# One small constant tile cut from 16 columns to 1, in a two-layer hybrid decoder trunk

## The chip, the cores and the metric

The kernel runs on one core of one Trainium2 chip. The metric is the device time of one execution, in microseconds (us), lower is better; the times shown are medians over several executions.

## The reference, cut to what matters

Two layers. Layer 0 mixes tokens with a chunked state-space scan, layer 1 with causal pooling windows. Each layer is followed by a gated feed-forward block with a causal depthwise convolution. Every sub-layer stands between two RMS normalisations. All is float32, 512 tokens of 1024 features.

```python
def rms_norm(x, w):
    xf = x.astype(jnp.float32)
    xf = xf * lax.rsqrt(jnp.mean(xf * xf, axis=-1, keepdims=True) + EPS)
    return (xf * w.astype(jnp.float32)).astype(x.dtype)
...
    for i in range(DEPTH):
        h = rms_norm(x, norm_mix_pre[i])
        ...
        x = x + rms_norm(mix, norm_mix_post[i])
        f = conv_ffn(rms_norm(x, norm_ffn_pre[i]), ffn_w_up[i], ffn_conv_w[i], ffn_conv_b[i],
                     ffn_w_down[i])
        x = x + rms_norm(f, norm_ffn_post[i])
```

The group norm inside the scan mixer uses the same EPS. The constant EPS = 1e-6 is what the changed tile holds.

## The kernel before

**Work and staging.** The weights stream through in slabs of 1 MB (8 KB per partition). SyncE loads a slab into `raw`. ScalarE copies it, rounded, to `w_hi` (line 261), VectorE subtracts to get the remainder `w_lo` (line 266), and TensorE multiplies in three passes, hi by hi, hi by lo and lo by hi, to keep float32 accuracy. The input projection, the gate and the up projections are `block_product` (lines 269 to 271), with slices of the weights as the stationary operand and `h_hi`/`h_lo` moving. The output and down projections are `rows_chunk` (line 874), where the stationary operand is `y_hi`/`y_lo` or `act_hi`/`act_lo` and the weights move.

**Stages in order of time.** Start and B/C projection (0 to 95 us of the profile), the scan over 16 head pairs (95 to 310), output projection (310 to 390), normalisations (390 to 435), up projection of layer 0 (435 to 666), down (666 to 764), normalisations and pooling mixer (764 to 843), up of layer 1 (843 to 1074), down (1074 to 1194), last normalisation and store. Every engine has a program written out by hand, in a fixed order, tied to the others by semaphores.

**The steps of the scan that the text names.** For each head pair: transposes of `xbc` (line 600), twelve products of `xde` and `cb_off` (line 646), sixteen of `xdt` and `decay` (line 655). `decay` is loaded by a DMA (line 547), then changed in place by VectorE (line 779), ScalarE (lines 694 and 699) and VectorE (`mask_dve`, line 786), which the products of line 655 wait for. Once for each group of four pairs there are the products of line 573. The normalisations transpose `stage` on TensorE (line 333). The causal taps of the convolutions are line 380: each reads a bank of PSUM and adds into `tmp[:, slot, back:]` with `back` 1, 2 or 3, so that the operand in SBUF begins 4, 8 or 12 bytes behind the start of its slot; the three forms are told apart by their lengths, 511, 510 and 509.

**The tile `eps`.** It is allocated as `[P, 16]`, filled once by GpSimd (line 1152), and read as `eps[:, 0:1]`, the bias of the square roots of lines 291, 314 and 730. Columns 1 to 15 are read by nothing. TensorE and ScalarE wait at the start for the four constants, of which it is one.

**Where tiles lie.** Tiles are placed in the order in which they are declared, one behind the other, and the start of each is rounded up to a multiple of 32 bytes per partition. In the compiled kernel before, `eps` lies at byte 118,400 of each partition and takes 64 bytes. All the tiles of the kernel, before and behind it, have sizes that are multiples of 64 bytes, and all begin at multiples of 64. Ahead of it lie `xres`, `h_hi`, `h_lo`, `raw`, `w_hi`, `w_lo`, `par`, `ident`, `upper` and `ones`. Behind it lie `tmp`, `pre_b`, `post_b`, the small tiles of the norms, the pooling windows, `xbc` and everything that shares memory with it in turn: `cb_diag`, `cb_off`, `xdt`, `xde`, `decay`, `from_start`, `gate`, `y_hi`/`y_lo`, `act_hi`/`act_lo`, `wf_hi`/`wf_lo`, `stage`, `wdt_*`. The sharing is by stacked scopes and by filler tiles of fixed size, all behind `eps`.

Of the kernel before, what the change touches and what calls it, by code (L numbers as in the profile page):

```python
# [10 lines left out]
P = 128  # L11
# [5 lines left out]
def hybrid_trunk(nc, x, ssd_w_in, ssd_conv_w, ssd_conv_b, ssd_dt_bias, ssd_a_log, ssd_d, ssd_norm_w,  # L17
# [75 lines left out]
    with ExitStack() as ctx:  # L93
        def sb(name, shape, dt=F32, scope=ctx):
            return scope.enter_context(nc.sbuf_tensor(name, shape, dt))
# [15 lines left out]
        ident = sb("ident", [P, P])  # L111
        upper = sb("upper", [P, P])
        ones = sb("ones", [P, P])
        eps = sb("eps", [P, 16])
        tmp = sb("tmp", [P, 4, T])
        pre_b = sb("pre_b", [P, D])
        post_b = sb("post_b", [P, D])
# [1353 lines left out]
```

## Time and profile before

| | |
|---|---|
| median of 3 runs | 1201.6 us (1200.21 to 1202.83) |
| the profiled execution's own time | 1202.83 us |
| its span, first to last instruction | 1201.1 us |
| PE / PEld / DVE / ACT / POOL busy | 96% / 81% / 56% / 44% / 3% |
| granted TensorE clock, mean | 0.987 of full |

The profiled execution is the slowest of the three runs, and its span is 1.7 us shorter than its time. PE is TensorE's matmuls, PEld its weight loads (they overlap the matmuls), DVE VectorE, ACT ScalarE, POOL GpSimd, and SPq the queue of SyncE, which issues the loads. In an engine's column "busy" counts instructions at work; a wait is told by the instruction that came late.

### The profile page before, as it was taken

To read this page: it belongs to the slowest core of one execution; us is meant where nothing else is said; L and a number is where in the kernel's file an instruction comes from. 1 tells how busy PE (TensorE), PEld (TensorE's weight loads), DVE (VectorE), ACT (ScalarE), POOL (GpSimd) and SP (SyncE) were. 2 spreads that over 40 slices of the span, in tenths; PEclk is the share of its full clock that TensorE was granted. 3 is DMA by queue.
4 is the path that set the end of the run, shared out by engine and by line. 5 is a ranking of instruction groups with operands and counts; after the bars stand their busy time and mean duration, and the time that the engine had idled before them with its cause. 6 is when DMAs were issued, how large, how long until landed. Compare 5 with 4: busy or idle time off the path is not lost.

```text
span 1201.1 us, 14740 instructions
## 1 busy us (share of the span) xinstructions
PE 1155.5 (96%) x5780; PEld 972.4 (81%) x5780; DVE 671.8 (56%) x766; ACT 523.0 (44%) x613; POOL 32.6 (3%) x87
## 2 busy tenths in 40 slices
PE   5999999999999899999999999998999999999997
PEld 5877888888788688888888888898888888888886
DVE  4567777878732746556565422466556566652124
ACT  4467666667532544434444211354434434441112
POOL 5000000000100000000000000000000000000000
PEclk9999999999999899999999999988999999999999
DMA  8142343433222303333222322402232332223211
GB/s 277 57 139 79 123 132 117 130 116 133 102 70 105 106 10 134 103 105 102 88 89 105 105 105 99 164 1 70 87 102 75 105 105 90 88 102 105 105 70 70
DMA packets 85227, 122.26 MB, mean 102 GB/s; under 512 B 4150, under 2 KB 71198, under 8 KB 85182
## 3 DMA queue, kind: packets, MB, share of 16 engines
q1 hardware_dynamic: 84592, 121.37, 30.1%
q8 instruction: 33, 0.54, 0.2%
q10 hardware_dynamic: 590, 0.25, 0.1%
q14 instruction: 12, 0.10, 0.0%
HBM read 119.44 MB, written 2.16 MB: 101 GB/s over the span
## 4 chain that ended last, share of the span: by engine, by line
PE 89%; DVE 5%; ACT 3%; DMA 1%; issue 1%; SPq 0%; DVEq 0%; ACTq 0%
PE bank L874 25%; PE bank L269 19%; PE bank L271 19%; PE bank L270 19%; PE bank L646 2%; DVE w_lo L266 2%; PE bank L655 1%; ACT w_hi L261 1%; DMA raw<-in_ssd_w_in 1%; DVE stage L301 1%; DVE xres L304 1%; PE bank L1035 1%; PE bank L600 1%; PE bank L333 1%; PE bank L573 1%
## 5 line engine op out<-in xcount | busy, mean ns | idle before, releaser
L269 PE MATMUL bank<-h_hi,w_hi 128*128 128x512 f32 (+1 forms) x1056 | 404.4, 383 | 11.1 <-DVE h_lo L345 7.7
L271 PE MATMUL bank<-h_hi,w_lo 128*128 128x512 f32 (+1 forms) x1056 | 400.2, 379 | 0.0
L270 PE MATMUL bank<-h_lo,w_hi 128*128 128x512 f32 (+1 forms) x1056 | 400.0, 379 | 0.0
L266 DVE TENSOR_TENSOR w_lo<-raw,w_hi 128x2048 fp32r<-128x2048 f32 x92 | 210.8, 2292 | 238.5 <-ACT w_hi L261 238.2
L380 DVE SCALAR_TENSOR_TENSOR tmp<-bank,par,tmp 128x511 f32<-128x511 f32 (+2 forms) x248 | 185.2, 748 | 129.4 <-ACT tmp L371 116.6
L261 ACT ACTIVATE w_hi<-raw 128x2048 fp32r<-128x2048 f32 x92 | 175.4, 1906 | 169.5 <-PE bank L874 152.3
L269 PEld LDWEIGHTS bank<-h_hi,w_hi 128*128 128x128 f32 x1056 | 201.5, 191 | 49.6 <-DVE w_lo L266 7.3
L271 PEld LDWEIGHTS bank<-h_hi,w_lo 128*128 128x128 f32 x1056 | 201.2, 191 | 36.8
L270 PEld LDWEIGHTS bank<-h_lo,w_hi 128*128 128x128 f32 x1056 | 201.6, 191 | 35.4
L371 ACT ACTIVATE tmp<-bank,par 128x512 f32<-128x512 f32 x112 | 86.8, 775 | 259.5 <-PE bank L271 259.3
L874 PE MATMUL bank<-w_hi,act_hi 128*128 128x512 f32 x352 | 109.1, 391 | 0.0
L874 PE MATMUL bank<-w_hi,act_lo 128*128 128x512 f32 x352 | 108.8, 390 | 0.0
L874 PE MATMUL bank<-w_lo,act_hi 128*128 128x512 f32 x352 | 108.8, 390 | 0.0
L874 PEld LDWEIGHTS bank<-w_hi,act_hi 128*128 128x128 f32 x352 | 66.5, 189 | 13.8
L874 PEld LDWEIGHTS bank<-w_hi,act_lo 128*128 128x128 f32 x352 | 66.4, 189 | 13.8
L874 PEld LDWEIGHTS bank<-w_lo,act_hi 128*128 128x128 f32 x352 | 66.4, 189 | 13.8
L993 ACT ACTIVATE act_hi<-tmp 128x512 f32 (+1 forms) x44 | 27.3, 634 | 58.6 <-DVE tmp L1008 58.6
L874 PE MATMUL bank<-w_hi,y_hi 128*128 128x512 f32 x128 | 40.8, 400 | 2.0 <-DVE w_lo L266 2.0
L874 PE MATMUL bank<-w_lo,y_hi 128*128 128x512 f32 x128 | 39.9, 394 | 0.0
L874 PE MATMUL bank<-w_hi,y_lo 128*128 128x512 f32 x128 | 39.8, 392 | 0.0
L990 ACT ACTIVATE tmp<-tmp 128x512 f32<-128x512 f32 x44 | 27.4, 627 | 25.6 <-DVE tmp L380 25.6
L345 DVE TENSOR_TENSOR h_lo<-bank,h_hi 128x512 fp32r<-128x512 f32 x32 | 20.7, 684 | 27.3 <-ACT h_hi L339 27.3
(161 smaller groups left out, 973.9 us busy)
## 6 DMA issues: line engine op xcount, KB each, us to landing
raw<-in_ffn_w_up SPq DMA_DIRECT2D x44, 1024.0 KB, 5.0
raw<-in_ffn_w_down SPq DMA_DIRECT2D x22, 1024.0 KB, 4.8
raw<-in_ssd_w_in SPq DMA_DIRECT2D x20, 1024.0 KB, 5.7
decay<-ac_dram SPq DMA_DIRECT2D x16, 512.0 KB, 3.8
raw<-in_ssd_w_out SPq DMA_DIRECT2D x8, 1024.0 KB, 4.9
from_start<-ac_dram SPq DMA_DIRECT2D x32, 128.0 KB, 3.7
xres<-in_x SPq DMA_DIRECT2D x4, 512.0 KB, 7.9
result<-xres SPq DMA_DIRECT2D x4, 512.0 KB, 2.6
```

The lines of the kernel that those rows point to most:

```text
L261: act.activation(w_parts(n, i)[0][:], raw[n % 2][:], ACT.Copy).then_inc(hi_ready, 1)
L266: dve.tensor_tensor(lo[:], raw[n % 2][:], hi[:].bitcast(F32), ALU.subtract).then_inc(lo_ready, 1)
L269: pe.matmul(dst, wh, xh, start=first, stop=False, **kw)
L270: pe.matmul(dst, wh, xl, start=False, stop=False, **kw)
L271: return pe.matmul(dst, wl, xh, start=False, stop=last, **kw)
L345: dve.tensor_tensor(h_lo[:, 4 * j:4 * j + 4, cs(c)], chunked(bank[:, 2 * c + j, :]), h_hi[:, 4 * j:4 * j + 4, cs(c)].bitcast(F32), ALU.sub ...
L371: act.activation(tmp[:, slot, :], bank[:, source, :], ACT.Identity, bias=b, scale=w).then_inc(conv_tap, 1)
L380: dve.scalar_tensor_tensor(tmp[:, slot, back:], bank[:, source, 0:T - back], w, tmp[:, slot, back:], ALU.mult, ALU.add).then_inc(conv_part ...
L646: mm = pe.matmul(bank[:, YO_BANK, cs(c)], xde[:, i, :], cb_off[p // QPG % 2][:, i, :], start=i == froms[0], stop=i == froms[-1])
L874: mm = pe.matmul(bank[:, 2 * c + j, :], x[:, cs(c)], w[:, k, j * T:(j + 1) * T], start=start, stop=stop)
L990: act.activation(tmp[:, j, :], tmp[:, j, :], ACT.Silu).then_inc(gate_silu, 1)
L993: act.activation(act_hi[:, bass.ds(2 * i + j, 1), :].rearrange("p a l -> p (a l)"), tmp[:, 2 + j, :], ACT.Copy).then_inc(act_hi_ready, 1)
```

## The change

`eps` becomes one column wide. The memset of line 1152 then writes one column. Nothing else in the source changes: not an instruction, a semaphore, a loop or a transfer. As the starts are rounded up to 32 bytes, `eps` takes 32 bytes in place of 64, and every tile behind it begins 32 bytes earlier: at 32 past a multiple of 64 instead of on one. All of them move by the same amount, so which tiles share memory stays as it was, and the ten named tiles ahead of `eps` don't move.

```diff
@@ -111,7 +111,7 @@
         ident = sb("ident", [P, P])
         upper = sb("upper", [P, P])
         ones = sb("ones", [P, P])
-        eps = sb("eps", [P, 16])
+        eps = sb("eps", [P, 1])
         tmp = sb("tmp", [P, 4, T])
         pre_b = sb("pre_b", [P, D])
         post_b = sb("post_b", [P, D])
```

## Rows read from the trace of the kernel before

**Rows 1.** The page: busy time of each engine, and the chain that ended last.

```profile
PE 1155.5 (96%) x5780; PEld 972.4 (81%) x5780; DVE 671.8 (56%) x766; ACT 523.0 (44%) x613; POOL 32.6 (3%) x87
...
PE 89%; DVE 5%; ACT 3%; DMA 1%; issue 1%; SPq 0%; DVEq 0%; ACTq 0%
PE bank L874 25%; PE bank L269 19%; PE bank L271 19%; PE bank L270 19%; PE bank L646 2%; DVE w_lo L266 2%; PE bank L655 1%; ACT w_hi L261 1%; DMA raw<-in_ssd_w_in 1%; DVE stage L301 1%; DVE xres L304 1%; PE bank L1035 1%; PE bank L600 1%; PE bank L333 1%; PE bank L573 1%
```

**Rows 2.** Windows, scan and last down projection: PE, PEld, DVE, ACT, POOL, clock, DMA.

```profile
95.00:310.00 215.00, 215.00 (x1244) 179.75 (x1246) 168.77 (x228) 146.10 (x166) 12.96 (x10) 1.00 0.37 121
...
1074.00:1194.00 120.00, 119.80 (x529) 98.90 (x527) 34.88 (x25) 26.77 (x24) 0.00 (x0) 1.00 0.23 85
```

**Rows 3.** Timeline of the first microseconds: start, duration, engine, line.

```profile
0.95 0.11 POOL L1152 MEMSET eps<- 128x16 f32 x1
...
2.90 0.10 POOL L1165 MEMSET win_first<- 128x1 f32 x1
...
4.79 1.28 ACT L312 ACT_TABLE_LOAD   x1 [4.79 <-DMA xres<-in_x]
```

**Rows 4.** Groups by line and form on VectorE: busy us, mean ns, idle before.

```profile
L380 DVE SCALAR_TENSOR_TENSOR tmp<-bank,par,tmp 128x510 f32<-128x510 f32 x112 | 83.9, 749 | 12.0 <-DVE tmp L380 2.7
L380 DVE SCALAR_TENSOR_TENSOR tmp<-bank,par,tmp 128x511 f32<-128x511 f32 x112 | 83.6, 746 | 116.6 <-ACT tmp L371 116.6
...
L1008 DVE TENSOR_TENSOR tmp<-tmp 128x512 f32<-128x512 f32 x44 | 28.3, 684 | 0.0
...
L304 DVE TENSOR_TENSOR xres<-xres,stage 128x1024 f32<-128x1024 f32 x16 | 19.6, 1225 | 0.6
L779 DVE TENSOR_TENSOR decay<-a_cum,decay 128x1024 f32<-128x1024 f32 x16 | 19.6, 1223 | 6.1 <-DMA decay<-ac_dram 6.1
L786 DVE TENSOR_TENSOR decay<-decay,cb_diag 128x1024 f32<-128x1024 f32 x16 | 19.5, 1219 | 0.9 <-ACT decay L699 0.9
...
L380 DVE SCALAR_TENSOR_TENSOR tmp<-bank,par,tmp 128x509 f32<-128x509 f32 x24 | 17.9, 748 | 0.8
...
L816 DVE SCALAR_TENSOR_TENSOR tmp<-xbc,d_pair,bank 128x512 f32<-128x512 f32 x16 | 11.9, 743 | 0.0
...
L819 DVE TENSOR_TENSOR tmp<-tmp 128x384 f32<-128x384 f32 x16 | 8.9, 558 | 0.5
```

**Rows 5.** One line on ScalarE: duration ns min/median/max, first and last start, form.

```profile
L314 ACT ACTIVATE rms_x<-ss_x,eps x16: 294/296/298, 8.6 to 829.9; 128x1 f32<-128x1 f32 x16
```

**Rows 6.** Weight load and matmul of line 874: duration ns min/median/max.

```profile
L874 PEld LDWEIGHTS bank<-w_hi,act_hi x352: 187/188/333, 665.9 to 1192.3; 128*128 128x128 f32 x176
L874 PE MATMUL bank<-w_hi,act_hi x352: 387/389/774, 666.1 to 1192.5; 128*128 128x512 f32 x176
```

**Rows 7.** The chain near the end: start us, us, what.

```profile
1149.83 43.99 PE bank L874 x194
```

**Rows 8.** The chain in the scan and at a transpose: start us, us, what.

```profile
101.01 1.34 PE bank L646 x12
102.34 1.02 PE bank L655 x16
...
109.05 0.44 PE bank L600 x4
...
136.95 2.16 PE bank L573 x8
...
426.39 0.87 PE bank L333 x8
```

**Rows 9.** DMA issues: KB each, median us from issue to landing.

```profile
decay<-ac_dram SPq DMA_DIRECT2D x16, 512.0 KB, 3.8
```

**Rows 10.** Timeline of one step of the scan: DVE, and PE's start on decay.

```profile
108.51 1.23 DVE L779 TENSOR_TENSOR decay<-a_cum,decay 128x1024 f32<-128x1024 f32 x1 [2.48 <-DMA decay<-ac_dram]
...
113.74 1.23 DVE L786 TENSOR_TENSOR decay<-decay,cb_diag 128x1024 f32<-128x1024 f32 x1 [0.19 <-ACT decay L699]
...
116.23 1.09 PE L655 MATMUL bank<-decay,xdt 128*64 128x128 f32 x16
```

## The prediction, made before the changed kernel ran

> **What bounds the kernel now.** I read the page first: TensorE's matmuls are busy for 96% of the span, and the chain that ended last lies on TensorE for 89% of it, on VectorE for 5% and on ScalarE for 3% [rows 1]. So a change of the time has to come through TensorE's own instructions, or through the 8% in which TensorE is waiting for a chain of VectorE and ScalarE work (the start, the normalisations between the stages, the tail). Then I read the windows by stage. In the scan TensorE is busy for all of its 215.00 us, VectorE for 168.77 and ScalarE for 146.10; in the last down projection TensorE is busy for 119.80 of 120.00 us and VectorE for 34.88 [rows 2]. VectorE and ScalarE could be slower there and nothing would show.
>
> **The change in two parts.** The source loses 15 columns that nothing reads. What can be felt is (a) a shorter memset and (b) that every tile declared behind `eps` begins 32 bytes earlier, at 32 past a multiple of 64. All instructions, their shapes, their order and their semaphores stay.
>
> (a) The memset of 16 columns takes 0.11 us, and a memset of one column 0.10 [rows 3], so 0.01 us goes. It lies at 0.95 us, while ScalarE's first work stands behind the first load of x until 4.79 us [rows 3], and TensorE's behind that. The cover is that load; if it were gone, the part would be worth 0.01 us. I take 0.
>
> (b) No row of before shows a large operand at 32 past 64. The price has to be bounded by the nearest rows, engine by engine.
>
> *VectorE.* Line 380 is the nearest, because its SBUF operand, read and written, begins 4, 8 and 12 bytes behind a multiple of 64: 746 ns for 511 elements, 749 for 510, 748 for 509. Line 816 is the same kind of instruction (one source in PSUM, one in SBUF) at a multiple of 64: 743 ns for 512 [rows 4]. An element costs (684 - 558) / 128 = 0.98 ns, from lines 1008 and 819, both in `tmp` [rows 4]. Brought to 512 elements the taps take 747, 751 and 751 ns, 4 to 8 ns over 743, at most 1.1%. Those are stranger starts than the one that comes, and the difference may be the code's own. Second, pairs of tiles: line 304 works on `xres` with `stage`, line 779 on `a_cum` with `decay`, line 786 on `decay` with `cb_diag`, and they take 1225, 1223 and 1219 ns for the same 1024 elements [rows 4]. The places of two operands against each other are worth at most 0.5%.
>
> *ScalarE.* Line 314 writes single columns of a small tile, one after another at steps of 4 bytes, and takes 294 to 298 ns in all 16 [rows 5]. That is a weak witness, since the tile is one column wide; I let VectorE's 1.1% stand as the upper end for ScalarE as well.
>
> What of it is on the path: of the chain's 8% on these two engines, 5% + 3% = about 96 us, the splits of the weights (lines 266 and 261, 2% + 1% on the page, about 36 us) work on tiles that don't move. Of the other 60 us, 1.1% is 0.7 us. The bounds are 0 and +0.7 us from the taps, and 0.5% either way, 0.3 us, from the pairs. I take 0, since a tap at 4 bytes and one at 8 differ by as much as either from an aligned one.
>
> *TensorE.* The big moving operands, `h_hi`, `h_lo`, `w_hi` and `w_lo`, lie ahead of `eps` and stay. What moves is the stationary operand of line 874 (`y_*`, `act_*`), those of a few first blocks (`wf_*`), and both operands of the short products of the scan and the transposes. For line 874 a load takes 188 ns [rows 6], and a matmul follows its predecessor every 43.99 us / 194 = 227 ns [rows 7], so a load has 39 ns, 21%, to grow in before the matmuls feel it. I know of no row with a stationary or moving operand halfway into 64 bytes. The lower bound is 0. For the upper one I suppose that TensorE reads in pieces of 64 bytes, an assumption: a row of 128 floats, 512 bytes, is 8 pieces from an aligned start and 9 from 32 bytes in, one eighth more. Line 874's load would take 212 ns and still be hidden under 227. The short products are not hidden; worked out under the rivals, they would add 8.0 us. I take 0 here too: nothing in the rows shows such a piece size, and every row in which an address phase can be seen, on the two other engines, shows at most 1.1%.
>
> *Loads into moved tiles.* `decay` lands 3.8 us after its issue [rows 9], and in one step VectorE waited 2.48 us for it; the mask of line 786 then ended at 113.74 + 1.23 = 114.97, and the products that wait for it began at 116.23 [rows 10]. So a load may land 1.26 us later, a third of its 3.8 us, before TensorE feels it. I take nothing for the loads.
>
> The Trainium skill has a rule on just this, on the page "DMA: Bandwidth & Descriptors", section "How a descriptor splits into AXI transactions": a descriptor that doesn't start at a multiple of 256 bytes pays for a whole first transaction. It tempts one to price a moved tile as dearer. But `decay` lay at 128 past a multiple of 256 before and lies at 96 past one after, so by that page its row of 4 KB goes from 132 beats to 131, which is an estimate of 1% off a transfer of 3.8 us and no loss. No row here shows a beat, and neither the sum nor a chance goes by it.
>
> **The sum.** 0.00 (memset) + 0.0 (VectorE and ScalarE) + 0.0 (TensorE) + 0.0 (loads) on the profiled execution's 1202.83 us. That one is the slowest of the three runs shown, 1.2 us over their median of 1201.6, for no reason that the change touches, so the forecast goes to the median: 1201.6 us.
>
> **The rivals.**
>
> *TensorE reads a half-shifted row slower: slower than before.* Places: each of the 16 steps of the scan has 1.34 us of line 646, 1.02 of line 655 and 0.44 of line 600 on the chain, 2.80 x 16 = 44.8 us; the four groups have 2.16 us each of line 573, 8.6 us; the three normalisations whose `stage` is transposed do so in four chunks each, 12 in all, at 0.87 us for the 8 transposes of line 333, 10.4 us [rows 8]. Together 63.8 us with nothing to hide behind, since TensorE is busy for the whole scan [rows 2]. One eighth more is 8.0 us, 1209.6 us. It decides from 2.4 / 63.8 = 3.8% more per product. For it: no row excludes it. Against it: it needs a piece size that nothing shows, and line 646 takes 1.34 us / 12 = 112 ns for 128 columns [rows 8], 0.87 ns each, where line 874 takes 227 / 512 = 0.44 ns [rows 7]: the short products get a column at half the pace at which columns are seen to come, so there is room for a longer read. In a harder form the loads of line 874 grow past 39 ns; there are 352 of them for each of the three passes of the two down projections [rows 6], 1056 in all, so that each nanosecond beyond costs 1.1 us.
>
> *A late load: slower.* If loads into tiles at 32 past 64 took half as long again, `decay` would land 1.9 us later, 0.64 us past the slack of 1.26. TensorE would stand 0.64 us in such steps; six of the sixteen loads made VectorE wait before, by 6.1 us in all [rows 4], so 3.8 us, 1205.4 us. It decides from about a third more, 1.26 us plus 0.4 us in six steps. Against it: the load writes whole kilobytes to each partition, so that a cut piece at either end is a small share.
>
> *Faster.* If moved and unmoved tiles stood in each other's way before, the shift could help. The pairs of rows 4 leave 0.5% for it, 0.3 us of 60. To reach 2.4 us it would take 4% off every VectorE and ScalarE instruction of the normalisations: 1199.2 us or less. Nothing speaks for it.
>
> *The change doesn't move anything.* If places were rounded to 64 bytes, the tiles would stay and the time with them: 1201.6 us. It ends where the forecast does.
>
> **How the numbers follow.** A difference of under 0.2%, 2.4 us, can't be told from no change for this kernel; its three runs are themselves 0.2% apart. The forecast, with the case in which nothing moves, has 0.81. TensorE slower has 0.08 and the late load 0.04, and 0.01 goes to a slower case that I haven't thought of: slower 0.13. Faster has 0.06. The band of no change, 1199.2 to 1204.0, holds 0.81 by itself; I open it to the bounds of the unknown costs, 0.3 + 0.4 us below (the pairs, and how far apart runs lie) and up to just past the late load, so 1198.5 to 1206.0.
>
> **What the profile after would show.** If I am right, lines 380, 816, 1008, 304 and 786 keep their means to within 1%, the load of line 874 stays at 188 ns, a step of the scan keeps 1.34, 1.02 and 0.44 us, `decay` lands in 3.8 us, the scan ends at the same microsecond and the tail from the last matmul to the last sum stays as it is. The prediction is wrong on TensorE if 1.34 and 1.02 grow, by an eighth in the rival; on the loads if VectorE's wait of 6.1 us for `decay` grows and line 655 starts to wait for the mask; on VectorE and ScalarE if the taps or the squares of the normalisations move by over 1%. If none of these moves and the time does, then something lies outside of what rows of instructions show.

## The result, and the profile after

The changed kernel takes 1206.86 us (median of 6, 1205.99 to 1207.80) against 1200.9 us for the kernel before (median of 6 on the same chip): a ratio of 1.0051, with a 95% interval of 1.0038 to 1.0064, 6.0 us slower. The forecast was 1201.6 us, no change, with a range of 1198.5 to 1206.0. It was wrong.

The profiled execution after has a span of 1204.4 us. These are its lines that answer to the page [rows 1] and to VectorE's and ScalarE's rows [rows 4, 5]. First the page, busy time of each engine:

```profile
PE 1157.6 (96%) x5780; PEld 965.7 (80%) x5780; DVE 671.7 (56%) x766; ACT 523.0 (43%) x613; POOL 32.6 (3%) x87
```

VectorE by line and form:

```profile
L380 DVE SCALAR_TENSOR_TENSOR tmp<-bank,par,tmp 128x510 f32<-128x510 f32 x112 | 83.9, 749 | 12.0 <-DVE tmp L380 2.7
...
L304 DVE TENSOR_TENSOR xres<-xres,stage 128x1024 f32<-128x1024 f32 x16 | 19.6, 1225 | 0.6
L779 DVE TENSOR_TENSOR decay<-a_cum,decay 128x1024 f32<-128x1024 f32 x16 | 19.6, 1222 | 7.3 <-DMA decay<-ac_dram 7.1
...
L816 DVE SCALAR_TENSOR_TENSOR tmp<-xbc,d_pair,bank 128x512 f32<-128x512 f32 x16 | 11.9, 742 | 0.0
```

The taps are at 749 ns as before, line 304 at 1225, line 779 at 1222 (1223 before), line 816 at 742 (743 before). At these places VectorE shows no change, nor does ScalarE: line 314 takes 294 to 295 ns (294 to 298 before). The loads of `decay` land in 3.9 us (3.8 before), and VectorE's wait for them is 7.1 us instead of 6.1. TensorE doesn't feel it: from its first products of line 646 to its first of line 874 the scan takes 209.5 us before and 209.4 after. The short products, where the prediction had its slower rival, are the same too, in the chain (start, duration, what):

```profile
100.60 1.34 PE bank L646 x12
101.94 1.02 PE bank L655 x16
...
136.53 2.15 PE bank L573 x8
...
427.93 0.87 PE bank L333 x8
```

What moved is the long products of line 874. The chain of the kernel before has three unbroken runs of them, one in the output projection and one in each down projection:

```profile
334.92 54.65 PE bank L874 x240
...
666.25 97.93 PE bank L874 x432
...
1074.12 119.69 PE bank L874 x528
```

The same three runs after:

```profile
334.68 56.02 PE bank L874 x240
...
667.51 100.81 PE bank L874 x432
...
1073.95 123.21 PE bank L874 x528
```

Duration by count is the pace: 97.93 / 432 = 226.7 ns before and 100.81 / 432 = 233.4 ns after, 6.7 ns more for each product, in both down projections alike. In the output projection 227.7 and 233.4, 5.7 ns more. The three runs alone are 7.8 us longer. The row of the weight loads, answering to [rows 6], says nothing of it, and the matmul's own duration shows it as 6 ns:

```profile
L874 PEld LDWEIGHTS bank<-w_hi,act_hi x352: 187/187/192, 667.1 to 1195.6; 128*128 128x128 f32 x176
L874 PE MATMUL bank<-w_hi,act_hi x352: 392/395/483, 667.4 to 1195.8; 128*128 128x512 f32 x176
```

The load's median went from 188 to 187 ns. Lines 269 to 271, whose operands lie ahead of `eps` except in the few products with `wf_*`, did not slow down.

Line 874 has 352 products with `act_*` and 128 with `y_*` in each of its three passes. The 1056 of the down projections pay 6.7 ns each, 7.1 us, and the 384 of the output projection 5.7 ns, 2.2 us: 9.3 us together. (The expectations below take 6.7 ns for all 1440 and so 9.6 us.) The median grew by 6.0. Both facts want an explanation: why the pace changed, and where 3.3 us came back.

### The profile page after: what moved, and what is told of

It is laid out like the page before. It is cut to its first block, busy times and chain, and to the rows that moved or that the text cites. A ratio compares the mean times of both kernels' runs of the same rounds, so it can differ in the third digit from the quotient of the medians.

```text
span 1204.4 us, 14740 instructions
## 1 busy us (share of the span) xinstructions
PE 1157.6 (96%) x5780; PEld 965.7 (80%) x5780; DVE 671.7 (56%) x766; ACT 523.0 (43%) x613; POOL 32.6 (3%) x87
## 4 chain that ended last, share of the span: by engine, by line
PE 90%; DVE 5%; ACT 3%; DMA 1%; issue 1%; SPq 0%; DVEq 0%; ACTq 0%
PE bank L874 25%; PE bank L269 19%; PE bank L271 19%; PE bank L270 19%; PE bank L646 2%; DVE w_lo L266 2%; PE bank L655 1%; ACT w_hi L261 1%; DMA raw<-in_ssd_w_in 1%; DVE stage L301 1%; DVE xres L304 1%; PE bank L1035 1%; PE bank L600 1%; PE bank L333 1%; PE bank L573 1%
## 5 line engine op out<-in xcount | busy, mean ns | idle before, releaser
L345 DVE TENSOR_TENSOR h_lo<-bank,h_hi 128x512 fp32r<-128x512 f32 x32 | 20.6, 684 | 23.9 <-ACT h_hi L339 23.9
```

Source lines behind the costliest of these rows:

```text
L345: dve.tensor_tensor(h_lo[:, 4 * j:4 * j + 4, cs(c)], chunked(bank[:, 2 * c + j, :]), h_hi[:, 4 * j:4 * j + 4, cs(c)].bitcast(F32), ALU.sub ...
```

## The experiments

All ratios are to the kernel before in runs on the same chip, with 95% intervals.

**e1: the narrow tile, with the places of before.** It parts the width of the tile from the places of its neighbours.

```diff
-        eps = sb("eps", [P, 16])
+        eps = sb("eps", [P, 1])
+        sb("pad", [P, 8])
```

> The tile eps stays one column wide, and a filler of 32 bytes stands behind it, so that every later tile lies where it lay before the change. If the change works through the places of tiles alone (my theory), the median is that of the kernel before, 1200.9 us within 2, and the products of line 874 go back from 233.4 to 226.7 ns apart. If the width of the tile, its memset or something unseen is the cause, it stays at 1206.9.

Measured: ratio 0.9998 (0.9987 to 1.0009). The run of 432 products takes 97.93 us again, to the digit. The change works through the places alone.

**e2: every tile moved by 32 bytes.** It tells an absolute rule from a relative one.

```diff
         bank = ctx.enter_context(nc.psum_tensor("bank", [P, 8, T], F32))
+        sb("pad", [P, 8])
         xres = sb("xres", [P, NCH, D])
```

> The kernel before, with 32 bytes of filler ahead of the first tile: every tile begins at 32 past a multiple of 64, weights and features as well. Theory A, absolute: a stationary row that begins halfway into 64 bytes costs 6.7 ns per product of 512 columns. Then the 2784 products of 512 columns of lines 269 to 271 slow down as well, 18.5 us, and line 874's 1440, 9.6 us: about 1229 us. Theory B, relative: what counts is where the stationary operand lies against the moving one, which this kernel leaves as it was in the kernel before: 226.7 ns for line 874 and 1200.9 us within 2.

Measured: ratio 1.0000 (0.9990 to 1.0010). Its chain:

```profile
334.31 54.69 PE bank L875 x240
...
665.18 97.93 PE bank L875 x432
...
1070.39 119.69 PE bank L875 x528
```

(Line 875 is line 874 of before: the filler is one line.) Every operand begins at 32 past a multiple of 64 and the pace is 226.7 ns. Theory A, the prediction's slower rival in general form, is out: here no product of TensorE pays for operands that begin halfway into 64 bytes. What counts lies between the two operands.

**e3: only `act_hi` and `act_lo` moved.** 32 bytes of filler ahead of them, nothing else.

```diff
+            sb("pad", [P, 8], scope=scope)
             act_hi = sb("act_hi", [P, FB, T], F32R, scope=scope)
```

> The kernel before, with 32 bytes of filler ahead of act_hi and act_lo alone: only the stationary operand of the two down projections (1056 products of line 874) lies at 32 past a multiple of 64, and y_hi, y_lo and wf stay. If the cost sits in the pair of stationary act and moving weights, the down projections go to 233.4 ns per product, +7.0 us, the output projection stays at 227.7, and the median is about 1207.9 us. If another moved tile is the cause, the time stays at 1200.9.

Measured: 1207.86 us against 1200.80, +7.1 us by the medians and 7.6 by the ratio of 1.0063 (1.0050 to 1.0076), where 1056 x 6.7 ns = 7.1. Inside one kernel, one pair of operands is slow and the other isn't:

```profile
335.36 54.69 PE bank L875 x240
...
666.88 100.81 PE bank L875 x432
...
1076.59 123.21 PE bank L875 x528
```

**e4: the tiles moved 32 bytes the other way,** `eps` of 24 columns.

> eps of 24 columns: everything behind it lies 32 bytes later than before, not earlier. If half of 64 bytes is what counts, line 874 goes to 233.4 ns as in the changed kernel and the median to about 1206.9 us. If the direction or the exact distance counts (128 or 256 bytes as the period), the pace is another one, 226.7 or in between.

Measured: ratio 1.0067 (1.0051 to 1.0082), 100.81 us for the 432 products. The direction doesn't matter.

**e5: moved by 64 bytes,** `eps` of 32 columns.

> eps of 32 columns: everything behind it moves by 64 bytes. If the distance between the stationary and the moving operand counts modulo 64 bytes, line 874 stays at 226.7 ns per product and the median at 1200.8 us. If it counts modulo 128 or 256 (the tiles lie at 128 past a multiple of 256 before), the pace becomes 233.4 ns or another one, and the median 1207 or more.

Measured: ratio 1.0054 (1.0036 to 1.0072), 100.81 us again, 233.4 ns. So 64 bytes is not the period, and the picture of "halfway into 64 bytes" is wrong even for the distance.

**e6: the weights `w_hi` and `w_lo` off.** They move by 32 bytes and everything behind them by 64.

```diff
         raw = [sb(f"raw{s}", [P, SLAB]) for s in range(2)]
+        sb("pad", [P, 8])
         w_hi = [sb(f"w_hi{s}", [P, SLAB], F32R) for s in range(2)]
         w_lo = [sb(f"w_lo{s}", [P, SLAB], F32R) for s in range(2)]
+        sb("pad2", [P, 8])
```

> Filler so that w_hi and w_lo alone lie at 32 past a multiple of 64 (the tiles behind them are moved by 64, a whole step), while h_*, act_* and y_* stay on multiples of 64. The weights are the stationary operand in lines 269 to 271 and the moving one in line 874. Theory B, relative: both kinds pay 6.7 ns for each product of 512 columns, 2784 + 1440 of them, +28 us, about 1229 us. A theory in which only a stationary operand off 64 pays: +18.5 us, 1219 us, and line 874 at 226.7. One in which only a moving operand off 64 pays: +9.6 us, 1210 us, lines 269 to 271 unchanged. All three allow 1 us less for the products of 256 columns.

Measured: 1222.28 us, ratio 1.0173 (1.0155 to 1.0190), +20.6 us by the medians. Line 874 (here 876) has them as the moving operand and takes 100.81 us for 432 products. Lines 269 to 271 have them as the stationary one and slow down too. The form of before and then that of e6, on the line of the second pass:

```profile
L270 PE MATMUL bank<-h_lo,w_hi 128*128 128x512 f32 x928 | 361.7, 390 | 0.0
```

```profile
L272 PE MATMUL bank<-h_lo,w_hi 128*128 128x512 f32 x928 | 367.4, 396 | 0.0
```

390 to 396 ns, as line 874 went from 389 to 395. With e2, in which both operands moved and nothing paid, neither operand matters by itself: both kinds of product pay when the distance between the two is off. The size was missed: the sum said 28 us and 21 came. Most of the gap is in the trace. From start to start the 2784 products of lines 269 to 271 go from 227.0 to 233.2 ns, 17.3 us in place of 18.5, and line 874 adds its 9.3. The products of 256 columns give back 2.0 us, among them those with `wf_*`, which lie 64 bytes off `h_*` here. (The expectation calls 64 bytes a whole step; e5 shows that it isn't one.) That leaves 24.6 us.

**e7 and e8: starts at 16 and at 4 bytes past a multiple of 64.** `eps` of 4 and of 1 column, with the rounding of the tiles' starts lowered to 4 bytes (and `xres` held in its place). `eps` took 64 bytes before and takes 16 and 4 now, so the tiles behind it move by -48 and by -60 bytes.

> eps of 4 columns with the rounding of tile starts lowered to 4 bytes: everything behind it lies at 16 past a multiple of 64, what is ahead stays. If any distance that isn't a multiple of 64 costs the same, 233.4 ns and about 1207 us. If the cost grows with the distance up to 32 bytes, half of it, 230 ns, 1204 us. If 32 bytes is special (two operands in opposite halves), 226.7 and 1200.8.

> eps of 1 column with no rounding: everything behind it lies 4 bytes past a multiple of 64. The same three answers as for 16 bytes: 233.4 ns and 1207 us if any distance costs, close to 226.7 and 1200.8 if the cost grows with the distance or is special to 32. VectorE and ScalarE now work in tiles at odd places: by the taps of before at most 1.1% each, not seen in the time.

Measured: e7, ratio 1.0042 (1.0027 to 1.0056), 100.17 / 432 = 231.9 ns. e8, ratio 1.0060 (1.0039 to 1.0080), 100.81 us, 233.4 ns. Both expectations count the distance from the next multiple of 64, and e5 took that away: against the kernel before the operands are 48 and 60 bytes off, not 16 and 4. Between 32 and 64 bytes the cost doesn't grow with the distance, 48 costs a little less than either. A distance under 32 bytes was not tried.

**e9 and e10: 128 and 256 bytes,** `eps` of 48 and of 80 columns.

> eps of 48 columns: everything behind it is moved by 128 bytes. In the kernel before all the large tiles begin at 128 past a multiple of 512, so that stationary and moving rows are congruent modulo 512. Theory B with a period of 512 bytes (the length of a stationary row of 128 floats): any other distance costs, line 874 at 233.4 ns, about 1207 us. With a period of 128: 226.7 ns and 1201.5 us.

> eps of 80 columns: everything behind it is moved by 256 bytes. Period 512: 233.4 ns, about 1207 us. Period 128 or 256: 226.7 ns and 1201.5 us.

Measured: 128 bytes, ratio 1.0040 (1.0026 to 1.0054), 100.40 / 432 = 232.4 ns; its output projection pays as much as that of the changed kernel, 55.99 us for 240. 256 bytes, ratio 1.0001 (0.9989 to 1.0012):

```profile
333.92 54.67 PE bank L874 x240
...
664.75 97.94 PE bank L874 x432
```

A distance of 256 bytes is as good as none. Of the shifts from 32 to 256 bytes it is the only free one, and so the period isn't the 512 that I had thought the likelier.

The first blocks of the up projection, products of 256 columns with `wf_*` stationary, go by another table. From start to start they take, by the median, 120.0 ns at a distance of 0 or 256, 118 at +32 and at -60, 117 at -32 and at -48, 113 at 64 and 119 at 128: they are faster off it. In the timeline (start, duration, engine, line) before:

```profile
441.68 0.28 PE L271 MATMUL bank<-h_hi,wf_lo 128*128 128x256 f32 x1
441.80 0.28 PE L269 MATMUL bank<-h_hi,wf_hi 128*128 128x256 f32 x1
441.92 0.28 PE L270 MATMUL bank<-h_lo,wf_hi 128*128 128x256 f32 x1
442.04 0.28 PE L271 MATMUL bank<-h_hi,wf_lo 128*128 128x256 f32 x1
```

and in e5, 0.34 us for three in place of 0.36:

```profile
441.55 0.28 PE L271 MATMUL bank<-h_hi,wf_lo 128*128 128x256 f32 x1
441.66 0.28 PE L269 MATMUL bank<-h_hi,wf_hi 128*128 128x256 f32 x1
441.78 0.28 PE L270 MATMUL bank<-h_lo,wf_hi 128*128 128x256 f32 x1
441.89 0.28 PE L271 MATMUL bank<-h_hi,wf_lo 128*128 128x256 f32 x1
```

**e11: only `wf_hi` and `wf_lo` off, by 64 bytes.** A 64-byte filler in front of the shared region, and 448 more in front of everything in it but `wf_*`.

```diff
+        sb("pad", [P, 16])
...
+        sb("pad_m", [P, 112], scope=mixer)
...
-            sb("gap_y", [P, 32 * KB], scope=scope)
+            sb("gap_y", [P, 32 * KB + 112], scope=scope)
...
-            sb("gap_f", [P, 16 * KB], scope=scope)
+            sb("gap_f", [P, 16 * KB + 112], scope=scope)
```

(and the same 112 columns ahead of `par_rows` and `act_hi` and in `gap_dt`.)

> A version meant to beat both: all tiles keep their distance of a multiple of 512 bytes (those in the shared region are moved by 512), except wf_hi and wf_lo, which lie 64 bytes past one. They are used only in products of 256 columns, 192 in the first blocks of the up projection and 96 in the pooling mixer, and those came every 120 ns at distance 0 and every 113 ns at a distance of 64. If the sign of the cost turns with the number of columns, line 874 stays at 226.7 ns, the 288 products take 7 ns less each, and the time is 2.0 us under the kernel before, about 1199.5 us (0.17%, at the edge of what can be measured). If the gain of the short products came from something else that moved with them, they stay at 120 ns and the time at 1201.5.

Measured: ratio 1.0016 (1.0003 to 1.0028), slightly slower, not faster. Line 874 stayed at 226.7 ns, but the 256-column products came every 118 ns, not 113. By the declarations `wf_*` and `h_*` lie at the same places here as in e5, which had 113, so for these products something else counts besides the distance. The expectation failed in its size and in the sign of the time. The mean granted clock was lower than in the kernel before beside it, 0.9872 against 0.9884, some 1.4 us in proportion.

**e12 and e13: the cost and its complement.** e12 puts only `y_*` and `act_*` 64 bytes off (576 more in `gap_y`, 1088 ahead of `act_hi`, 1024 in `gap_f` and `gap_dt`). e13 puts all the rest behind `eps` off and those two back on a multiple of 256.

```diff
-        eps = sb("eps", [P, 16])
+        eps = sb("eps", [P, 32])
...
-            sb("gap_y", [P, 32 * KB], scope=scope)
+            sb("gap_y", [P, 32 * KB + 48], scope=scope)
...
+            sb("pad_a", [P, 112], scope=scope)
...
-            sb("gap_f", [P, 16 * KB], scope=scope)
+            sb("gap_f", [P, 16 * KB + 64], scope=scope)
```

> Only the stationary operands of line 874 are put off the 256-byte distance: y_* and act_* lie 64 bytes past a multiple of 256 from the weights, stage and the tiles behind it are moved by 1024 (a whole number of periods), the rest stays. If line 874's 1440 products at 6.7 ns each are the whole cost, +9.6 us: 1210.8 us. The changed kernel showed only +6 with the same 1440 products slower, so in it 3 us must have come back elsewhere; if that giving back belongs to the other moved tiles it is missing here (1210.8), and if it comes from the slower products themselves (later or steadier work of TensorE) it is here too (1207.5).

> The complement, and a version that could beat both: everything behind eps lies 64 bytes off (stage and what follows it 320), except y_* and act_*, which are put back to a multiple of 256 from the weights. Line 874 at 226.7 ns. If the other moved tiles give time back, the stretch between the two down projections takes 305.6 us as in the changed kernel and not 307 to 310, and the first blocks run at 113 ns: 1197.0 to 1198.5 us. If the giving back came from the slower products, only the 288 products of 256 columns gain, up to 2 us: 1199.2 to 1201.2.

Measured: e12 1207.42 us, ratio 1.0058 (1.0043 to 1.0074); e13 1201.31 us, ratio 1.0008 (0.9998 to 1.0017). The down run of layer 0, first in e12 and then in e13, shows that each edit did what it was meant to:

```profile
667.53 100.81 PE bank L875 x432
```

```profile
666.00 97.94 PE bank L875 x432
```

The slow products alone give as large a ratio as the whole change (1.0051), and the other moved tiles alone give nothing back in the time, though the 256-column products ran at 113 ns in e13. Its stretch between the two down projections, which the expectation put at 305.6 us if moved tiles gave time back, took 310.3. So the 3 us are no gain from moved tiles, but for some 0.7 us that the faster products with `wf_*` are worth in the changed kernel (192 at 3 ns, 96 at 1.3).

The mean granted clock goes along with that. In single executions it lies between 0.987 and 0.991 in the 23 executions of the kernel before beside e1 to e4, with a mean of 0.9888, at 0.9914 in the 7 executions of the changed kernel, and at 0.9905 in the 6 of e12. 0.26% of 1200 us is 3.1 us; going by the kernel before itself, 1200.8 us at 0.988 (8 executions) and 1198.8 at 0.991 (5), it is an estimate of 1.7. So 9.3 - 0.7 comes down to between 5.5 and 6.9 us, and 6.0 was measured. At one and the same clock more of the cost shows: the executions at 0.991 have a mean of 1206.6 us for the changed kernel (4) and 1198.8 for the kernel before (5), 7.8 us apart. One place where it differs in the profiles is the start of the pooling mixer. The window of 784 to 794 us, before:

```profile
784.00:794.00 10.00, 10.00 (x40) 8.85 (x41) 5.16 (x6) 2.53 (x5) 0.00 (x0) 0.66 0.01 2
```

and after:

```profile
784.00:794.00 10.00, 8.52 (x54) 7.28 (x53) 9.01 (x12) 5.26 (x11) 0.00 (x0) 1.00 0.01 2
```

The third number from the end is the granted clock: 0.66, TensorE at half of its 2.4 GHz for two thirds of the window, against 1.00. The stretch between the end of the first down run and the start of the second is 309.9 us before and 305.6 after (from the starts and durations of the chain above). But the window holds other work after, since each step comes some 4 us later, and e12, with the same slow products, had 0.70 there in its profile and a stretch of 307.5. One profile isn't the proof; the clocks of all executions carry the statement. They also show that slower down projections alone don't bring the higher clock: e3 had them, and its five executions have a mean of 0.9878, under the 0.9888 of the kernel before. That fits with e3 having paid its whole 7.1 us. The eight kernels whose output projection is slow as well (the changed one, e4 to e9 and e12) lie at 0.9894 to 0.9914, and all the others at 0.9872 to 0.9891. No kernel with the output projection alone slow was run, and why the clock was higher stays open.

## Why the prediction was wrong

**What bounds the kernel** was read rightly. A change had to come through TensorE's own products or the 8% of glue, and it came through the products.

**(a) the memset** fell from 0.11 to 0.10 us, unseen, as said.

**VectorE, ScalarE and the loads** were right: the bound from the taps and from the pairs of tiles held, the means of VectorE's lines stayed within 1 ns of where they were, and line 314 on ScalarE within 2 ns.

**TensorE: this is the step that failed.** The term of the sum was 0.0, and its products got slower by 9.3 us in sum, of which 6.0 reached the time. The prediction wrote "I take 0 here too: nothing in the rows shows such a piece size, and every row in which an address phase can be seen, on the two other engines, shows at most 1.1%". Two things were wrong in it. It carried over to TensorE what VectorE's rows show. And it asked only whether a row that begins off a boundary takes longer to read. For VectorE the question of two operands against each other had been asked, with three pairs of tiles; for TensorE, which reads a stationary and a moving operand at once, it wasn't. The front of the document says that the ten tiles ahead don't move and the rest does, which is that question nearly put: line 874 is the one product of 512 columns with an operand on either side of `eps`. The prediction also counts the transposes among the products whose operands both move. They don't: `ident` lies ahead of `eps`.

**The cover of 39 ns** was wrong as an argument. The load of line 874 was held to be hidden unless its duration of 188 ns grew by 39. Its duration didn't grow at all, and the products came 6.7 ns later each. Room between a load's duration and the pace did not protect the pace.

**The slower rival** had the sign and missed the mechanism and the place. It put 8.0 us on the short products of the scan and the transposes, which did not change, and took line 874 as covered. Its absolute rule, in the form that the expectation of e2 gives it, would have made e2 some 28 us slower, and e2 was equal. The chance of 0.13 for slower was too low for a kernel with 96% of TensorE and no row at the new places.

**The Trainium skill** was used in the prediction for the loads alone, and nothing hung on it. A page that bears on the failed step is "SBUF — State Buffer", section "SBUF: two separate sides": it says that on the engines' side only the port pair which VectorE and GpSimd share makes anyone wait, and that TensorE never does. That is said of one engine against another, and it would be wrong to read from it that TensorE's pace can't depend on where its own operands lie: in e3, moving `act_*` by 32 bytes with all else in place took it from 226.7 to 233.4 ns. What inside the chip makes it so no run here shows.

## What to carry to other kernels

A tile's size is also the place of every tile behind it. Where a long run of products of 512 columns has its stationary and its moving operand in different tiles, write down the distance between their starts, and after any edit to a small tile, filler or constant ahead of one of them check that it is still a multiple of 256 bytes; here that is worth 3% of each 512-column product. Read the pace of a run of products from the chain, duration by count, since neither the load's duration nor the page's busy share shows such a change. And when no row of the trace shows the state after the change, ask for each engine what it reads at the same time, and leave more than 13% on the side on which there is no evidence.

## What the runs showed of the hardware

The pace of products of 128 rows and 512 float32 columns (in the rounded format of `w_hi`) depends on the distance between stationary and moving operand within a partition. Counted from the places of the kernel before, where all large tiles are whole multiples of 512 bytes apart, the down projections took 226.7 ns at 0 and 256 bytes (before, e1, e2, e10), 233.4 at 32 either way, at 64 and at -60 (after, e4, e5, e8), 231.9 at -48 (e7), 232.4 at 128 (e9). At 2.4 GHz 226.7 ns are 544 cycles, 32 over the 512 columns, and 233.4 are 560, 48 over.

Products of 256 columns went the other way, 120 ns at 0 and 113 to 119 off it, but in e11 a distance that gave 113 ns in e5 gave 118 with the other tiles in place, so for them more than the pair's distance counts. That was not followed up. Of 128 columns the runs show the transposes of line 333: `stage` moved and `ident` stayed, by -32 bytes in the changed kernel, 64 in e5, 128 in e9 and -60 in e8, and each time 8 of them took 0.87 us, 109 ns each, as before. The products of line 646 (1.34 us for 12) had both operands moved in these kernels, so of them the runs say nothing about the distance.

A slower pace did not cost its whole sum: 6 to 7 us of 9.3 in the changed kernel and e12, and 21 of 24.6 in e6, while moving `act_*` alone cost all of its 7.1. The granted clock was 0.2 to 0.3% higher than before in the first two, 0.1% lower with `act_*` alone, and in e6 0.9900 against 0.9881. There it is 2.3 us in proportion, an estimate that leaves 22.3 us, within the 18.6 to 22.8 of e6's interval.

No version tried beats the kernel before: e1, e2, e10 and e13 are equal to it within their intervals, and e11 is slower by 0.16% (0.03 to 0.28).
